# The value projection of a neighbourhood attention, cut into 16 blocks of 128 tokens, twelve of them placed between the pairs of heads

## The reference, cut to what matters

```python
q, k, v = jnp.split(h_lat @ w_qkv, 3, axis=-1)       # 16 heads of 64
qc, kc, vc = jnp.split(h_ctx @ w_qkv, 3, axis=-1)
...
s_loc = jnp.where(col_valid, q*scale . k + bias, NEG_INF)   # 4 rows x 16 columns of neighbours
s_ctx = q*scale . k_ctx
p = softmax(concat(s_loc, s_ctx))
o = p_loc @ v_blk + p_ctx @ v_c
y_l = o @ w_o
```

## Time and profile before

| | |
|---|---|
| median of 3 runs | 1831.51 us (1830.14 to 1832.6) |
| span of the profiled execution | 1827.1 us |
| the profiled execution's own time | not recorded; its span lies 4.4 us under the median of the runs |
| TensorE matmuls busy | 1765.4 us (97%) |
| TensorE weight loads busy | 1506.7 us (82%) |
| VectorE busy | 1195.2 us (65%) |
| ScalarE busy | 726.4 us (40%) |
| the four value tiles and the attention | 1496.6 to 1596.5 us of the span |

### The profile page before, as it was taken

One profiled execution on the slowest core, in us unless ns is written; L12 is line 12 of the kernel. 1 busy time (PEld: TensorE's weight loads), 2 busy tenths in 40 slices (PEclk: granted clock), 3 DMA queues, 4 the chain that ended last, 5 costly groups with the idle time before them and its releaser, 6 DMA issues.

```text
span 1827.1 us, 25749 instructions
## 1 busy us (share of the span) xinstructions
PE 1765.4 (97%) x9970; PEld 1506.7 (82%) x9970; DVE 1195.2 (65%) x1896; ACT 726.4 (40%) x1033; POOL 62.5 (3%) x41
## 2 busy tenths in 40 slices
PE   7999999999998899999999999999999999999998
PEld 5777888888886588888888888888888898689998
DVE  4688678778999746776677367766333534855554
ACT  4433123337788734222222242222222433844343
POOL 0000000030000010000000200000002000010001
PEclk8999999999999999999999999999999999999999
DMA  8487568332221123544554235445223341034543
GB/s 335 185 321 281 180 224 310 134 115 87 104 94 69 47 93 116 209 170 155 201 190 152 99 144 203 166 155 178 104 77 104 136 178 70 2 138 178 190 175 124
DMA packets 48024, 282.98 MB, mean 155 GB/s; under 512 B 5424, under 2 KB 6704, under 8 KB 23888
## 3 DMA queue, kind: packets, MB, share of 16 engines
q1 hardware_dynamic: 47952, 282.03, 42.4%
HBM read 268.37 MB, written 13.63 MB: 154 GB/s over the span
## 4 chain that ended last, share of the span: by engine, by line
PE 78%; DVE 12%; ACT 5%; issue 3%; DMA 1%; POOL 0%; DVEq 0%; ACTq 0%; SPq 0%; POOLq 0%
PE ps_all L1900 24%; PE ps_all L1904 24%; PE ps_all L1901 24%; DVE w_lo L1141 2%; DVE mod_junk L1161 2%; DMA mod_raw<-in_w_mod 1%; ACT w_hi L640 1%; PE ps_all L1896 1%; PE banks L2464 1%; DVE sq_acc L1630 1%; PE banks L2058 0%; PE banks L1997 0%; PE banks L2283 0%; DVE gated L1187 0%; PE ps_all L2096 0%
## 5 line engine op out<-in xcount | busy, mean ns | idle before, releaser
L1900 PE MATMUL ps_all<-a_hi,w_lo 128*128 128x512 f32 (+1 forms) x1832 | 652.2, 356 | 7.3 <-DVE w_lo L1141 3.0
L1904 PE MATMUL ps_all<-a_lo,w_hi 128*128 128x512 f32 (+1 forms) x1832 | 647.4, 353 | 2.0 <-DVE a_lo L1306 1.2
L1901 PE MATMUL ps_all<-a_hi,w_hi 128*128 128x512 f32 (+1 forms) x1832 | 646.4, 353 | 0.0
L1141 DVE TENSOR_TENSOR w_lo<-w_raw,w_hi 128x2048 fp32r<-128x2048 f32 (+2 forms) x173 | 351.2, 2030 | 149.6 <-ACT w_hi L640 149.5
L640 ACT ACTIVATE w_hi<-w_raw 128x2048 fp32r<-128x2048 f32 (+2 forms) x173 | 294.6, 1703 | 319.7 <-PE ps_all L1904 307.2
L1900 PEld LDWEIGHTS ps_all<-a_hi,w_lo 128*128 128x128 f32 x1832 | 346.5, 189 | 62.1 <-DVE w_lo L1141 9.0
L1904 PEld LDWEIGHTS ps_all<-a_lo,w_hi 128*128 128x128 f32 x1832 | 345.7, 189 | 51.7 <-DVE a_lo L1306 2.6
L1901 PEld LDWEIGHTS ps_all<-a_hi,w_hi 128*128 128x128 f32 x1832 | 346.1, 189 | 46.8 <-issue 0.2
L1161 DVE SCALAR_TENSOR_TENSOR mod_junk<-mod_raw,cond 128x1024 bf16<-128x1024 f32 x256 | 302.7, 1220 | 11.2 <-DMA mod_raw<-in_w_mod 5.6
L1900 PE MATMUL ps_all<-g_hi,w_lo 128*128 128x512 f32 (+1 forms) x734 | 261.5, 356 | 1.2 <-DVE w_lo L1141 1.2
L1901 PE MATMUL ps_all<-g_hi,w_hi 128*128 128x512 f32 (+1 forms) x734 | 259.7, 354 | 0.0
(11 more groups left out here) (280 smaller groups left out, 1523.2 us busy)
## 6 DMA issues: line engine op xcount, KB each, us to landing
w_raw<-in_tiles SPq DMA_DIRECT2D x112, 1024.0 KB, 4.8
mod_raw<-in_w_mod SPq DMA_DIRECT2D x64, 1024.0 KB, 4.9
w_raw<-in_tiles SPq DMA_DIRECT2D x32, 768.0 KB, 4.1
w_raw<-in_tiles SPq DMA_DIRECT2D x32, 640.0 KB, 3.8
start_w<-in_w_start SPq DMA_DIRECT2D x8, 1024.0 KB, 19.3
scaled<-in_split SPq DMA_DIRECT2D x12, 512.0 KB, 4.7
parts<-normed SPq DMA_DIRECT2D x12, 512.0 KB, 2.7
parts<-sq SPq DMA_DIRECT2D x12, 512.0 KB, 3.0
```

What stands on the lines that cost most here:

```text
L1141: nc.vector.tensor_tensor(w_lo[:, slot, 0:size], w_raw[:, slot, 0:size], w_hi[:, slot, 0:size].bitcast(F32), ALU.subtract).then_inc(lo_rea ...
L1900: pe.matmul(dst, w[1], x[0], start=start, stop=False)
L1901: pe.matmul(dst, w[0], x[0], start=False, stop=False)
L1904: return pe.matmul(dst, w[0], x[1], start=False, stop=stop_)
```

## The change

The value projection is cut into its 16 blocks (`value_part(i)`, tile `i // 4`, tokens `i % 4`). Block 0 stays where it was, blocks 1 to 3 go between the first scores, and blocks 4 to 15 stand in TensorE's loop, one at the end of each of the pairs 1 to 12. All blocks go to one PSUM bank, `bank[1]`, two of them side by side, and ScalarE copies it after every second one (`keep_values(i)`, 8 copies of 128 x 512 in place of 4 of 128 x 1024). Because the projection still reads `a_hi` and `a_lo` while outputs come out, the attended values go to `mix_hi` and `mix_lo`, which are declared in a scope of their own behind the attention's, and so lie on the addresses of `q_t` and `k_t`; `na_out` reads them there. The outputs of all but the last pair of heads use `bank[0]`. The splits of the value tiles 2 and 3 and of `na_out`'s first tile move into the loops at pairs 1, 5 and 9. The masking of the bias is moved: pieces 0 and 1 behind the splits 6 and 7, pieces 2 and 3 to VectorE's pairs 2 and 3, with a second semaphore for the second half of the bias. SyncE's order of DMAs is as it was.

```diff
+        with ExitStack() as mixed:
+            mix_hi = sbuf("mix_hi", [P, KT, NLAT], F32R, mixed)
+            mix_lo = sbuf("mix_lo", [P, KT, T], F32R, mixed)
...
+        def attention_out(tile, b, e):
+            return bank[1 if tile == PAIRS // 2 - 1 else 0][:, b:e]
+        def value_block(j):
+            return j + 3 if 1 <= j <= 12 else None
+        def value_split(j):
+            return {1: 2, 5: 3, 9: 4}.get(j)
...
# ScalarE
+                def keep_values(i):
+                    j, half = i // 2, i % 2
+                    if half == 0:
+                        act.wait_ge(N["values"], j + 1)
+                    else:
+                        act.wait_ge(pe_done, BASE["na_v"] + j + 1)
+                    nc.scalar.activation(v_tok[:, 2 * half:2 * half + 2, j * 256:(j + 1) * 256],
+                                         bank[1].rearrange("p (b c) -> p b c", b=2), ACT.Copy
+                                         ).then_inc(ps_free[j % 2] if half else N["kept"], 1)
...
+                split_hi(BASE["na_v"] + 1, 2048, 1)
+                keep_values(0)
+                exps(0)
                 for j in range(PAIRS):
                     if j + 1 < PAIRS:
                         exps(j + 1)
+                    if value_split(j):
+                        split_hi(BASE["na_v"] + value_split(j), 2048, value_split(j) % 2)
+                    if j == 0:
+                        keep_values(1)
+                    if value_block(j - 1) is not None and value_block(j - 1) % 2:
+                        keep_values(value_block(j - 1) // 2)
                     copy_turned(j)
                     if j >= 2 and j % 2 == 0:
                         high(j // 2 - 1)
...
# VectorE, in its loop behind scale_probs(j + 1)
+                    if value_split(j):
+                        split_lo(BASE["na_v"] + value_split(j), 2048, value_split(j) % 2)
+                    if j in (2, 3):
+                        masked(j)
...
# TensorE
+            def attended_tile(j):
...
+                for k in range(KT):
+                    if j == 0:
+                        pe.wait_ge(na_sem["mix"], k + 1)
+                    for m in range(2):
+                        mm = three(ps[slot][:, m, NCTX:T], [x[:, k, m] for x in w], (mix_hi[:, k, :], mix_lo[:, k, 0:NLAT]),
                                    k == 0, k == KT - 1)
+            def value_part(i):
+                j, t = i // 4, i % 4
+                n, slot = BASE["na_v"] + j, j % 2
+                if t == 0:
+                    pe.wait_ge(lo_ready, n + 1)
+                if t == 0 and j:
+                    pe.wait_ge(ps_free[1 - slot], (n - 1) // 2 + 1)
+                if t == 2:
+                    pe.wait_ge(na_sem["kept"], j + 1)
+                w = [x[:, slot].rearrange("p (k f) -> p k f", k=KT) for x in (w_hi, w_lo)]
+                o = bank[1][:, (t % 2) * 256:(t % 2) * 256 + 256]
+                for k in range(KT):
+                    mm = three(o, [x[:, k, t * P:(t + 1) * P] for x in (a_hi, a_lo)], [x[:, k] for x in w],
+                               k == 0, k == KT - 1)
+                if t == 1:
+                    mm.then_inc(na_sem["values"], 1)
+                if t == 3:
+                    mm.then_inc(pe_done, 1)
...
                 def outputs_of(j):
                     tile, s, at = pair_of(j)
                     pe.wait_ge(N["copied"], j + 1)
-                    if s == 0 and tile >= 2:
-                        pe.wait_ge(N["mix"], tile - 1)
+                    pe.wait_ge(ps_free[(tile // 2) % 2], (BASE["na_v"] + tile // 2) // 2 + 1)
+                    if s == 0 and 1 <= tile < PAIRS // 2 - 1:
+                        pe.wait_ge(N["mix"], tile)
...
-                for j in range(3):
-                    value_tile("na_v", j)
+                value_part(0)
+                for slot in range(2):
+                    pe.wait_ge(ps_free[slot], BASE["na_v"] // 2)
                 scores_of(0)
-                value_tile("na_v", 3)
-                pe.wait_ge(ps_free[0], BASE["na_out"] // 2)
+                value_part(1)
                 scores_of(1)
+                value_part(2)
                 scores_of(2)
-                pe.wait_ge(ps_free[1], BASE["na_out"] // 2)
+                value_part(3)
                 for j in range(PAIRS):
                     turn_probs(j)
                     if j:
                         outputs_of(j - 1)
                     if j + 3 < PAIRS:
                         scores_of(j + 3)
+                    if value_block(j) is not None:
+                        value_part(value_block(j))
                 outputs_of(PAIRS - 1)
```

More of the change, by code:

```diff
@@ L1066, in mixer1 @@
                 norm(4)
-                for segment in ("na_k", "na_q", "na_v"):
+                for segment in ("na_k", "na_q"):
                     for j in range(4):
@@ L1778, in mixer1, with masked @@
                 window = const[:, C_WINDOW:C_WINDOW + GRID_W].rearrange("p (a c) -> p a c", a=1).broadcast_to([P, 24, GRID_W])
[L1779 to L1786, removed]
+                def masked(x):
+                    dve.wait_ge(N["bias" if x < 2 else "bias_rest"], 16)
+                    at = slice(24 * x, 24 * x + 24)
+                    nc.vector.tensor_tensor(b[:, at], b[:, at], window, ALU.min).then_inc(N["masked"], 1)
+                for x in range(1, 9):
+                    split_lo(BASE["na_k"] + x + 1, 2048, (x + 1) % 2)
+                    if x >= 6 and x < 8:
+                        masked(x - 6)
                 def maxima(j):
@@ L1812, in low @@
                     nc.vector.tensor_tensor(
[L1813 to L1815 removed]
+                        mix_lo[:, tile, 0:NLAT].rearrange("p (r c) -> p r c", c=GRID_W),
+                        attention_out(tile, 0, NLAT).rearrange("p (r c) -> p r c", c=GRID_W)[:, :, ::-1],
+                        mix_hi[:, tile, :].bitcast(F32).rearrange("p (r c) -> p r c", c=GRID_W),
                         ALU.subtract).then_inc(N["mix"], 1)
[L1818 removed]
                 maxima(0)
@@ L2396, in pair_tile_from, with pair_tile @@
                 mm.then_inc(pe_done, 1)
-            def pair_tile(segment, j, K, at, before=None, t0=0, rows=None):
+            def pair_tile(segment, j, t0=0):
                 n, slot = BASE[segment] + j, j % 2
@@ L2402, in pair_tile @@
                 pe.wait_ge(ps_free[slot], n // 2)
[L2403 to L2406, removed]
+                w = [x[:, slot].rearrange("p (k m f) -> p k m f", k=KT, m=2) for x in (w_hi, w_lo)]
+                for k in range(KT):
                     for m in range(2):
-                        mm = three(ps[slot][:, m, t0:T], [x[:, k, m] for x in w],
-                                   (a_hi[:, at + k, rows or slice(t0, T)], a_lo[:, at + k, rows or slice(t0, T)]),
-                                   k == 0, k == K - 1)
+                        mm = three(ps[slot][:, m, t0:T], [x[:, k, m] for x in w], (a_hi[:, k, t0:T], a_lo[:, k, t0:T]),
+                                   k == 0, k == KT - 1)
@@ L2463, in outputs_of @@
                             head = 2 * tile + n
-                            mm = pe.matmul(bank[tile % 2][64 * n:64 * n + 64, s * P:(s + 1) * P],
+                            mm = pe.matmul(attention_out(tile, s * P, (s + 1) * P)[64 * n:64 * n + 64],
                                            v_tok[:, t, 64 * head:64 * head + 64], prob_t[:, at + n, t * P:(t + 1) * P],
```

31 lines of the change are left out of this document (12 added, 19 removed).

## The result

| | before | after |
|---|---|---|
| median (lowest to highest), 11 runs each | 1830.83 us (1829.77 to 1832.6) | 1835.22 us (1831.85 to 1836.49) |
| span of the profiled execution | 1827.1 us | 1834.3 us |
| mean granted clock (share of 2.4 GHz) | 0.9886 | 0.9885 |

The ratio is 1.0022, with a 95% interval of 1.0014 to 1.003: the interval excludes 1, and the changed kernel is slower by some 4 us. The forecast was 1834.0 us. I cut both traces at the same four marks: the first value matmul, the first `na_out` matmul, the first sum of norm 5 on TensorE (line 2096 of the changed kernel, 2058 of the one before) and the first matmul of `ffn3`.

The account below looks back on a forecast made before the run. TensorE was taken to bound the attention, VectorE close behind. Removing 3.97 us of gaps and adding waits, seams and a slower `na_out` summed to +2.5 us: 1834.0 us, range 1830.8 to 1836.8.

Parts of the forecast that it names:

- likeliest case: Whole kernel: the forecast of +2.5 us, within the 3.7 us a measurement tells apart; chance 0.50.
- gaps of before: TensorE's standstill at the two ends of the attention goes away: -3.97 us, the ceiling of the gain.
- gaps at the new end: Pairs 13 to 15, without a block: transposes 14, the last outputs and transposes 15 wait, together +0.83 us.
- ScalarE's split at pairs 5 and 9: `split_hi` ahead of `keep_values` delays the copy outputs 4 and 8 need: 1.6 us each, +3.2 us.
- entering the blocks: TensorE's seam into value matmuls, 15 entries instead of one, 0.10 us each: +1.40 us.
- leaving for transposes: TensorE's seam from a value block to transposes, 13 times at 0.03 us: +0.39 us (0 to 1.82).
- Rival 2: No wait at pairs 5 and 9, so -0.7 us in all, 1830.8 us; chance 0.08.
- Rival 3: Each block is left for transposes through a bare weight load, 0.14 us each: +3.9 us, 1835.4 us; chance 0.20.
- Rival 1: Seams between value blocks and other TensorE work are free: +0.6 us, 1832.1 us; chance 0.14.
- The last gap: Before transposes 15, which wait for ScalarE's copy 13, exponentials 15 and copy 14: +0.45 us.
- `na_out`: Its 192 matmuls go at 0.120 us instead of 0.118 because `mix_hi` and `mix_lo` start elsewhere: +0.40 us.
- sign of being wrong: `na_out`'s first matmul starting earlier than before, or gaps in the pairs without a split.

Follow-up runs that it names:

- e1: Changed kernel with ScalarE's split of pairs 1, 5 and 9 moved behind `copy_turned`; 1830.81 us, ratio 0.9999 to the kernel before.
- e5: e4 with the twelve value blocks in six visits of two and splits at pairs 4 and 8 instead of 5 and 9; 1837.9 us, ratio 1.0038.
- e3: Changed kernel with 448 unused bytes a partition ahead of `mix_hi`, run twice; 1831.44 and 1832.13 us, ratios 0.9999 and 1.0011.
- e4: Changed kernel with both the later split of e1 and the spare bytes of e3, run twice; 1827.1 and 1826.85 us, ratios 0.998 and 0.9989.
- e6: e4 with 24 more matmuls (2.88 us) in value tiles 1 and 2, run twice; 1830.4 and 1830.48 us, ratios 0.9996 and 1.0003.
- e2: Kernel before with twelve more matmuls in value tile 1, their results overwritten; 1832.52 us, ratio 1.0012.

## Why the prediction was right, and where not

The time lay in the range (1830.8 to 1836.8), 1.2 us above the forecast. The likeliest case, a loss too small to tell, came out at its upper edge: the first ratio is 1.0022, the other two 1.0031 and 1.0028, so slower by a little over 0.2% is the truer reading, and the 0.26 given to it was too little.

Step by step for the stage:

| term | forecast | measured |
|---|---|---|
| gaps of before | -3.97 | -3.97, all gone |
| gap at the new start | +0.15 | +0.12 |
| gaps at the new end | +0.83 | +0.69 |
| ScalarE's split at pairs 5 and 9 | +3.2 | +3.57 (e1) |
| entering the blocks | +1.40 | +1.40 (0.22 at the second matmul) |
| leaving for scores | +0.09 | +0.09 |
| leaving for transposes | +0.39 | -0.65 (13 x 0.97 instead of 1.02) |
| sum | +2.09 | +1.25; the stage: +1.19 |

- *The wait at pairs 5 and 9* was right in its place, its cause and nearly its size; e1 took it away and the stage lost 3.57 us. Rival 2 is out. It alone is why a change with 3.97 us to gain loses: the other terms of the stage come to -2.4.
- *Leaving for transposes* was the term with the wrong sign. I set it at +0.03 each, between 0 and 0.14, with no gain as the lower end; the transposes behind a block are 0.05 shorter than those behind scores. Rival 3 is out by the 0.12 us to the first transpose: its load, which that rival held to be bare, is the one that starts 0.10 us early. Rival 1 is half true: leaving for transposes is free, entering is not (0.10), nor is leaving for scores (0.09). In and out together cost 0.04 us in e5 (0.10 - 0.05 by the timeline), where rival 1 says 0 and the forecast 0.13.
- The rule of the Trainium skill, page TensorE: Matmul & The Clock Gate, section Step-by-step: what each phase is for, that the next weight load is pulled ahead under the matmul in flight, is borne out at the exits to transposes (the load 0.10 us ahead of its matmul, 0.12 from the last value matmul to the first transpose) and not at the entries (no load ahead of the scores, 0.22 to the second matmul).
- *The last gap:* 0.23 where I had 0.45. ScalarE's chain is the one of the forecast, but I counted whole durations where the next instruction begins some 0.1 us before the one ahead of it ends: copy 13 starts at 1594.29 with 1.02 us, the exponentials behind it at 1595.21, copy 14 at 1596.56 (forecast 1596.79), and the transposes at 1597.64 (1597.88).
- *`na_out`* at the slower pace was right, and e3 shows that the address is the cause. The term was undersized: e3 gives 1.25 us for 192 matmuls, 0.94 of it by the first sum of norm 5. The 0.1178 us of the trace that I read is not what the kernel before always does; its second trace has 0.1134.
- *The rest of the time* had no step at all. Stage and `na_out` give +2.1 us; measured are +4.4 to +4.5. The forecast came near the time because its sum of 2.5 was 0.4 too high in one part and lacked this other one: the agreement within 1.2 us is in part luck. The start of `na_out`, which the forecast put at 1598.5 us, came at 1600.93; 3.29 of that is the chance in front of the stage, and without it the start is 1597.64.
- *Signs and small readings.* The splits, the blocks and the pace came as forecast, the waits as 1.78 us for 1.6, but with no ScalarE copy named as the releaser. Neither sign of being wrong came: `na_out` does not start earlier than before, and the pairs without a split show no gaps but those at the two ends. The 14 us that blocks 1 to 3 were to cover are 12.1 by the forecast's own prices and 12.29 in the trace (1502.84 to 1515.13), still more than enough.

What is shown of that missing part: in fourteen traces the rest is 201.2 to 202.3 us when the low-clock stretch behind norm 5 is 3.4 or 6.8 us, seven times, and 204.3 to 206.0 when it is 10.2 or 13.7, seven times. So a long stretch goes with some 3 us. The dividing line becomes clear when only the part of the stretch that falls behind the first `ffn3` matmul is counted, from the rows of the granted clock in the traces: 2.9 to 4.1 us in the seven, 8.7 to 9.6 in the other seven, whatever lies before it in the norm, where TensorE stands still for about half of the time. That is 5.8 us more on average, of which half is lost at half the clock: an estimate of 2.9 of the 3.4 us between the two groups. The first 576 matmuls of `ffn3` carry most of it: 71.5 to 72.1 us in the one group, 73.6 to 74.6 in the other. The last layer carries a little more: all seven traces with the long stretch wait there for a weight tile (0.5 to 1.3 us), where the other seven wait 0 to 0.5 us, and the two of the kernel before not at all. In the changed kernel's first trace it is:

```profile
1807.49 0.38 PE L1938 MATMUL ps_all<-g_hi,w_lo 128*128 128x256 f32 x1 [1.31 <-DVE w_lo L1172]
```

The executions that were not profiled say something too, since each has its mean granted clock on record, to three places. The time that an execution lost to the low clock, its time times one less that clock, averages 22.0 us over the 23 executions of the changed kernel and 21.5 over e1's 11, against 19.7 to 19.8 in e3, e4 and e6 (23 each) and 20.9 in 89 of the kernel before, with standard errors of 0.2 to 0.4. So the two kernels with the unaligned `mix_hi` lose some 2 us more to the low clock than the aligned ones, on the average of all executions and not only in the traces. Against the kernel before it is about 1 us of the changed kernel's 2.4; where in the execution it falls, these figures do not say.

What is not settled: why the changed kernel and e1, the two with the unaligned `mix_hi`, had the long stretch in all four traces and lie 2.0 to 2.4 us above what stage and `na_out` give, while the others lie within 1.1 of it on either side and had the long one in three of ten. The stage's length is not the cause (e3 and e4 had both, each at one length). It may be the end of `na_out` at the slower pace; chance in four draws would explain the traces, but hardly the averages above. No run changed the address in the kernel before, which would have told.

## What to carry to other kernels

When work is interleaved into a pipeline that has no holes, the gain is at most the holes at its ends. Before anything else, walk each queue through one turn: an instruction that waits for the turn just ended must stand behind everything that the next turn wants. Here one `split_hi` two lines too early, twice, turned 2.4 us of gain in the stage into 1.2 of loss. And after moving a buffer, look at the pace of those who read it: 448 unused bytes a partition were worth 0.9 us of `na_out` and 1.25 by the first matmul of `ffn3`, and with the split's new place they made the fastest kernel of the study.

## What the runs showed of the hardware that I had not expected

- The pace of fp32r matmuls of 256 columns hangs on where the moving rows start: 0.1199 us each with `mix_hi` and `mix_lo` 64 bytes past a multiple of 512 (four traces), 0.1134 with them 448 bytes further, on a multiple (seven traces). The shift of 448 bytes is certain, the multiples are worked out from the order of declarations, and no other shift was run. The kernel before, also on a multiple, had 0.1178 once and 0.1134 in two traces of the same `na_out` code (e2's among them), so there is a second cause besides, which no run shows.
- Transposes take 0.97 us behind fp32r blocks and 1.02 behind scores. Behind a block their first weight load starts 0.10 us early; behind scores it starts with its matmul (0.00), and so does that of a block behind scores.
- A wait of TensorE can cost twice: each 2.7 us wait of e5 was followed by 3.4 us at 1.2 GHz. The 1.8 us waits of the changed kernel at the same places left the clock at 1.00.
- The same kernel, with the same stage to 0.03 us, came out of norm 5 with 3.4 us at 1.2 GHz in one execution and 10.2 or 13.7 in another.
